# Two-layer mixer trunk: wide and narrow matmuls of the feature chunks interleaved

## The reference

```
parts = split(x @ w_in)            # retention, latent attention, mLSTM, memory attention, gate z
y     = concat([ret, mla, mls, memo]) * silu(z)
x     = layernorm(ALPHA * x + y @ w_out) * g + b
```

## Time and profile before

| | us |
|---|---|
| median of 3 runs | 928.38 (928.37 to 928.53) |
| the profiled execution | 928.28 |
| its span, first to last instruction | 926.5 |
| TensorE busy | 910.5 (98%) |
| weight loads busy | 788.2 (85%) |
| VectorE busy | 647.7 (70%) |
| ScalarE busy | 502.3 (54%) |

### The profile page before, as it was taken

One profiled execution on the slowest core, in us unless ns is written; L12 is line 12 of the kernel. 1 busy time (PEld: TensorE's weight loads), 2 busy tenths in 40 slices (PEclk: granted clock), 3 DMA queues, 4 the chain that ended last, 5 costly groups with the idle time before them and its releaser, 6 DMA issues.

```text
span 926.5 us, 13958 instructions
## 1 busy us (share of the span) xinstructions
PE 910.5 (98%) x4980; PEld 788.2 (85%) x4980; DVE 647.7 (70%) x1292; ACT 502.3 (54%) x949; POOL 16.0 (2%) x18
## 2 busy tenths in 40 slices
PE   8999999999999999999999999999999999999994
PEld 6888998888888888888988889888888888888894
DVE  6878677776765775665669687766577567777657
ACT  6664765544555555544576556754354555555441
POOL 0000000000000000000000000000000000000001
PEclk9999999999999999999999999999999999999998
DMA  9785545655455556553765765565355554665743
GB/s 343 263 319 171 159 135 198 216 171 173 145 160 159 163 170 191 191 195 115 248 204 166 279 214 174 142 201 180 114 151 149 176 162 155 182 187 181 284 138 124
DMA packets 51861, 172.55 MB, mean 186 GB/s; under 512 B 6216, under 2 KB 6352, under 8 KB 51152
## 3 DMA queue, kind: packets, MB, share of 16 engines
q1 hardware_dynamic: 51792, 171.66, 56.6%
HBM read 169.53 MB, written 2.11 MB: 185 GB/s over the span
## 4 chain that ended last, share of the span: by engine, by line
PE 95%; DVE 2%; DMA 1%; ACT 1%; issue 0%; SPq 0%; DVEq 0%; ACTq 0%
PE acc L1187 22%; PE acc L1175 17%; PE acc L1176 17%; PE acc L1179 17%; PE acc L1193 11%; PE work L909 2%; DMA raw<-in_w 1%; PE work L1051 1%; PE work L969 1%; PE work L1011 1%; PE work L914 1%; PE work L916 1%; PE work L915 1%; DVE X L1677 1%; PE work L1086 1%; PE work L1087 1%
## 5 line engine op out<-in xcount | busy, mean ns | idle before, releaser
L1245 DVE TENSOR_TENSOR lo<-raw,hi 128x512 fp32r<-128x512 f32 (+2 forms) x624 | 393.3, 646 | 252.8 <-ACT hi L887 245.2
L887 ACT ACTIVATE hi<-raw 128x512 fp32r<-128x512 f32 (+2 forms) x624 | 363.2, 594 | 314.4 <-PE acc L1179 164.7
L1175 PE MATMUL acc<-hi,xx 128*128 128x512 f32 (+2 forms) x592 | 219.3, 375 | 0.0
L1176 PE MATMUL acc<-hi,xx 128*128 128x512 f32 (+2 forms) x592 | 211.3, 362 | 0.0
L1187 PE MATMUL acc<-xx,hi 128*128 128x512 f32 x768 | 211.1, 396 | 0.0
L1179 PE MATMUL acc<-lo,xx 128*128 128x512 f32 (+2 forms) x592 | 166.1, 362 | 0.0
L1187 PEld LDWEIGHTS acc<-xx,hi 128*128 128x128 f32 x768 | 131.3, 189 | 17.6
L1193 PEld LDWEIGHTS acc<-xx,lo 128*128 128x128 f32 x768 | 117.7, 189 | 16.4
L1176 PEld LDWEIGHTS acc<-hi,xx 128*128 128x128 f32 x592 | 111.7, 189 | 15.0
L1175 PEld LDWEIGHTS acc<-hi,xx 128*128 128x128 f32 x592 | 111.6, 189 | 15.0
L1193 PE MATMUL acc<-xx,lo 128*128 128x256 f32 x768 | 122.0, 281 | 0.0
(11 more groups left out here) (293 smaller groups left out, 1011.8 us busy)
## 6 DMA issues: line engine op xcount, KB each, us to landing
raw<-in_w SPq DMA_DIRECT2D x255, 512.0 KB, 3.7
raw<-in_w SPq DMA_DIRECT2D x50, 256.0 KB, 2.8
raw<-in_w SPq DMA_DIRECT2D x16, 328.0 KB, 3.2
Y<-in_wuq SPq DMA_DIRECT2D x2, 1152.0 KB, 8.0
Y<-in_x_t SPq DMA_DIRECT2D x4, 512.0 KB, 8.0
X<-in_x SPq DMA_DIRECT2D x4, 512.0 KB, 4.6
gb<-in_gb SPq DMA_DIRECT2D x1, 2048.0 KB, 7.3
Y<-in_gb SPq DMA_DIRECT2D x1, 2048.0 KB, 10.4
```

Of the source, the lines that this page charges most:

```text
L887: act.activation(place(l, t, hi), raw[:, s, (t % 2) * w:(t % 2 + 1) * w], ACT.Copy)\
L1175: pe.matmul(o, ah[:, q], hi[:, s, 0:w], start=k == 0, stop=False)
L1176: pe.matmul(o, al[:, q], hi[:, s, 0:w], start=False, stop=False)
L1245: dve.tensor_tensor(place(*at, lo), raw[:, s, (t % 2) * w:(t % 2 + 1) * w], place(*at, hi).bitcast(F32), ALU.subtract).then_inc(lo_done.se ...
```

## The change

In the feature chunks each low-weight matmul now directly follows the high-weight one of the same block, and the wait for the low tile stands after the slot's first wide matmul.

```diff
                                 q = slice(kk * FEAT + j * P, kk * FEAT + (j + 1) * P)
                                 pe.matmul(acc[:, p, j, :], hi[:, s, q], x, start=k == 0 and kk == 0, stop=False,
                                           skip_group_check=True)
-                        pe.wait_ge(lo_done.sem, lo_done.at(l, t))
-                        for kk in range(2):
-                            for j in range(2):
-                                q = slice(kk * FEAT + j * P, kk * FEAT + (j + 1) * P)
-                                m = pe.matmul(acc[:, p, j, 0:SEQ], lo[:, s, q], both_parts[:, 2 * k + kk, 0, :], start=False,
+                                if kk == 0 and j == 0:
+                                    pe.wait_ge(lo_done.sem, lo_done.at(l, t))
+                                m = pe.matmul(acc[:, p, j, 0:SEQ], lo[:, s, q], x[:, 0:SEQ], start=False,
                                               stop=2 * k + kk == KT - 1, skip_group_check=True)
                     m.then_inc(tile_used.sem, 1)
```

## The result

The changed kernel takes 930.1 us (median of 22 runs, 929.22 to 930.57) against 928.66 us (22 runs, 928.16 to 929.25); the ratio is 1.0016, with an interval of 1.001 to 1.0022. It is slower by 0.16%, where 925.9 was forecast.

The account below looks back on a forecast made before the run. TensorE's matmul spacing was taken to bound the kernel; 3.1 us gained from the new order less 0.7 us for the earlier wait gave -2.4 us, from 928.38 to 925.9 us, range 922.5 to 932.5 us.

Parts of the forecast that it names:

- What bounds the kernel: Whole kernel: TensorE, busy 98% of the span at 2.4 GHz; start-to-start spacing counts, a record less 162 to 163 ns.
- The spacing of the new order: Feature slots: alternating wide and narrow takes 346.7 ns a pair, 1386.7 ns a slot instead of 1403.3, gaining 3.1 us.
- Two of the ways: Pair estimates: uniform stretches gave 226.7+120 = 346.7 ns, averages by position gave 230+116.6 = 346.6 ns.
- the hole: Expected sign in TensorE's row: idle at 38.9 to 39.6 us before one slot's first narrow matmul, none elsewhere.
- rival B: Feature slots: every wide dear after a narrow, narrows 120 ns, pair 354 to 356; 932.4 to 934.2 us, chance 0.17.
- the additive rule: Feature slots: wide before narrow about 4 ns shorter, after narrow 1 longer; narrow after wide 2 shorter; pair 346.6 ns.
- How many slots have it to give: Feature slots: 168 gain 16.6 ns each, 56 beside jobs, at some 1392 ns, gain 5 each; 3.1 us.
- The wait: Layer 0 slot at 38.72 us: the earlier wait for low weights stalls TensorE once, costing 0.7 us outright.
- rival A: Feature slots: spacing does not care for the order, only the wait's cost remains; 928.9 us, chance 0.34.

Follow-up runs that it names:

- the other orders: The kernel before with seven other orders of a slot's eight matmuls in 13 feature chunks and WWNNWWNN in the rest; 928.94 us in a single execution.
- the wait alone: The kernel before with only the low-tile wait moved behind the slot's first wide matmul, order still four wide, four narrow; 928.83 us against 928.56, ratio 1.0002.
- TensorE alone: A kernel without the reference's computation, only stretches of matmuls from SBUF with no other engine at work; alternating pairs took 353.3 or 346.7 ns.

## Why the prediction was right or wrong

**What bounds the kernel**, and how a spacing is read from records: right. Record less 162 gave the spacing in every kernel.

**The spacing of the new order: the step that failed.** The prediction asked "what a pair takes" as though that were one number, found 346.7 by two ways ("Two of the ways meet at 346.7, so I take that: 1386.7 ns a slot") and gave it to all slots. The number is exact where it holds, down to 230+116.6 in the stretch of 51.8 us, but it is one of two settled values, and 130 of 224 slots (171 where the hole does not come) run at the other. The slow pair, 353.3, is close to rival B's 354 to 356; B's mechanism (a wide one behind a narrow one is always dear, 234 to 236) has the mean of the wides right (236.3) and that of the narrows wrong (117.0, not 120). With 1413.3 ns on average in 171 slots, 1386.7 in 48 and the other five near 1400, the change costs where it was to gain: +1.4 us in place of -3.1. The warning stood in the prediction's own rows: token chunks settle to 226.7 in one place and 233.3 in another, and the text said so; it was used as a bound for the mean and not as a sign that one order can have several rhythms. Averaging by position over slots that had not settled was the second mistake: the additive rule it gave is refuted by the other orders (1400 to 1413 for equal counts of changes).

**How many slots have it to give.** The slots beside jobs were taken to be at 1392 and to lose 5 ns. In the change those of the z chunks and of layer 1's memk rise instead: the 16 of memk average some 1404, against 1392 before (with 80 ns for each early start). A small term with the wrong sign, for the same reason. The 1392 fits those 16; over all 56 the starts of before give some 1395 (an estimate, by the same 80 ns), which would have put 0.2 us more into the gain.

**The wait.** Place, cause and moment were right: one slot, low weights at 39.40, the load at 39.45. The size was 0.46 and not 0.7, mainly since the seven slots ahead lost 0.08 us instead of gaining 0.1, so that TensorE came later, at 38.87. In another execution it was not there at all, and the wait alone could not be told from nothing by time (1.0002). That it costs "outright" was wrong in kind: where it came, the rhythm behind it was the fast one, which gave back more than it took.

**The totals.** The range of 922.5 to 932.5 held the time. The forecast and its largest chance (0.41 for 925.9) were on the wrong side; slower had 0.19 by more than 0.2%, and the 0.16% measured lies within the "same" of 0.41. The range held because it was wide enough to take in rival A and the cheaper half of B, not because the mechanism held; no rival had two values for one order. The rule of the Trainium skill in "TensorE: Matmul & The Clock Gate" ("Back-to-back issue gap"), which that section gives for an isolated matmul, would have had the order matter nothing, at 1300 ns a slot (an estimate from its formula). In TensorE alone the same four-and-four takes 1403 ns for eight, and the order moves it from 1387 to 1413, so the measurements decide against it on both counts.

## What to carry to other kernels

In a dense stream like this one the order of two widths is worth up to 2% of the stream (1387 to 1413 ns), in either direction, with no wait and no idle time to be seen: compare starts over a long uniform stretch, and ask whether the spacing is one value or several before multiplying it by a count. A mean over short, unsettled stretches does not forecast a settled one. If the spacing depends on how a stretch is entered, choose an order with a single value (here WWNN), or try the entries and read the result from the whole kernel's own starts. A small kernel with TensorE alone gave the same two values, but not the same entries: behind a settled four-and-four chunk the whole kernel went fast, the small one slow. And profile more than one execution: the shortest one need not be the usual one.

## What the runs showed of the hardware that was not expected

- Alternating fp32r matmuls of 512 and 256 columns have two stable rhythms, 346.7 and 353.3 ns a pair, at the full 2.4 GHz in both. Four-and-four has one (1403.3 for eight) and two-and-two one (1393.3). All are TensorE's own: they appear with every other engine silent.
- Four matmuls of 264 columns in front of an alternating stretch turned it from slow to fast for its 24 pairs, where one, two or three did not; behind a stall of 0.46 us it was fast for 40 slots, and slow in two executions without the stall.
- The settled values found (226.7, 233.3, 346.7, 353.3, 1393.3, 1400, 1406.7, 1413.3) differ by multiples of 6.7 ns. Four-and-four fits that only over the two slots after which its starts repeat (2 x 1403.3 = 2806.7). What in the engine has that step, and why the stationary operand in the B buffers costs a wide matmul 6.7 ns more, was not tried and stays open.
